# Eight modulation steps move to the first output stage, and two output tiles begin inside the recurrence

## The reference, cut to what matters

```python
mod = silu(cond) @ mod_w[l] + mod_b[l]            # cond: one vector for context, one for latent
sh_a, sc_a, g_a, sh_f, sc_f, g_f = split(mod, 6)
hn = rms_norm(x, norm_mix_g[l]) * (1 + sc_a) + sh_a
out = hybrid_mixer(hn) if l == 0 else rec_mixer(hn)   # l = 1: gated recurrence, 8 heads, two directions
x = x + g_a * out                                 # out ends in a matmul with a 1024 x 1024 matrix
hn = rms_norm(x, norm_ffn_g[l]) * (1 + sc_f) + sh_f
x = x + g_f * expert_choice_ffn(hn)               # each of 16 experts takes its top tokens
```

## Time and profile before

| view | what it gives |
|---|---|
| runs | median 4249.28 us (4249.1 to 4249.85) |
| the profiled execution | own time 4253.98 us, span 4252.2 us |
| PE, matmuls | 3907.3 us busy (92%) |
| DVE | 1762.6 us busy (41%) |
| ACT, POOL | 1120.3 us (26%), 221.8 us (5%) |

### The profile page before, as it was taken

The page is one execution under the profiler, slowest core; times in us unless marked ns, Lnnn a source line. Parts: engine busy times, 40 slices in busy tenths (PEclk is TensorE's granted clock), DMA queues, the critical chain, the costliest instruction groups (busy, mean ns, idle before and its releaser), DMA issues. The chain is left out here.

```text
span 4252.2 us, 56364 instructions
## 1 busy us (share of the span) xinstructions
PE 3907.3 (92%) x24019; PEld 3156.4 (74%) x24019; DVE 1762.6 (41%) x2924; ACT 1120.3 (26%) x2147; POOL 221.8 (5%) x277
## 2 busy tenths in 40 slices
PE   7998989999599999998899999999869599999998
PEld 3443456654499999997788888888744499999997
DVE  3224457755411111111468778888855411111112
ACT  3000024533211111100444555444522211110112
POOL 1120000000000000000000000000000000000000
PEclk9999989999799999999899999999979799999999
DMA  5552110013478888884210000110213578888887
GB/s 187 169 207 90 43 50 1 1 54 116 163 244 255 263 254 263 253 257 147 88 28 28 29 29 23 28 34 19 101 58 112 168 246 257 259 255 264 252 257 241
DMA packets 508361, 615.84 MB, mean 145 GB/s; under 512 B 17994, under 2 KB 468220, under 8 KB 502352
## 3 DMA queue, kind: packets, MB, share of 16 engines
q1 hardware_dynamic: 479808, 500.01, 36.5%
q0 software_dynamic: 25056, 101.61, 8.1%
q10 hardware_dynamic: 3248, 10.62, 0.6%
HBM read 559.02 MB, written 53.17 MB: 144 GB/s over the span
## 5 line engine op out<-in xcount | busy, mean ns | idle before, releaser
L1732 PEld LDWEIGHTS moe_pgu<-step_hnT,expert_w 128*128 128x128 f32 x8192 | 1118.0, 191 | 16.5 <-issue 16.5
L1732 PE MATMUL moe_pgu<-step_hnT,expert_w 128*128 128x160 f32 x8192 | 1125.7, 300 | 3.4 <-ACT step_hnT L1772 3.4
L1835 DVE TENSOR_TENSOR moe_hT<-moe_sg,moe_pgu 128x160 f32<-128x160 f32 x256 | 82.2, 321 | 1004.8 <-PE moe_pgu L1732 995.0
L1744 PE MATMUL moe_pol<-expert_w,moe_hT 128*128 128x256 f32 x2048 | 457.5, 381 | 2.3 <-DVE moe_hT L1835 1.0
L2034 PE MATMUL rec_pz<-step_hnT,rec_w 128*128 128x256 f32 x1920 | 424.5, 380 | 3.5 <-ACT l_zc L2106 1.9
L1744 PEld LDWEIGHTS moe_pol<-expert_w,moe_hT 128*128 128x128 f32 x2048 | 383.2, 190 | 59.0 <-DVE moe_hT L1835 9.9
L1783 ACT ACTIVATE moe_sg<-moe_pgu 128x160 f32<-128x160 f32 x256 | 77.8, 304 | 1301.4 <-PE moe_pgu L1732 1301.4
L2034 PEld LDWEIGHTS rec_pz<-step_hnT,rec_w 128*128 128x128 f32 x1920 | 362.7, 191 | 52.0 <-ACT l_zc L2106 2.3
L2038 PE MATMUL rec_pz<-rec_w,step_hnT 128*128 128x256 f32 x1280 | 288.2, 384 | 15.1 <-ACT rec_zg L2109 15.1
L2038 PEld LDWEIGHTS rec_pz<-rec_w,step_hnT 128*128 128x128 f32 x1280 | 243.9, 193 | 50.6 <-ACT rec_zg L2109 17.9
L2064 PE MATMUL rec_pg<-rec_ring 128*128 128x128 f32 x1600 | 196.9, 282 | 47.6 <-DVE rec_AT L2361 19.9
(11 more groups left out here) (391 smaller groups left out, 4456.0 us busy)
## 6 DMA issues: line engine op xcount, KB each, us to landing
expert_w<-in_moe_w_gu SPq DMA_DIRECT2D x256, 1024.0 KB, 10.5
expert_w<-in_moe_w_down SPq DMA_DIRECT2D x128, 1024.0 KB, 13.7
late_w<-in_mod_w POOLq DMA_DIRECT2D x40, 1024.0 KB, 5.2
rec_w<-in_r_w_in SPq DMA_DIRECT2D x40, 512.0 KB, 4.0
scratch_xm<-op_x ACTq DMA_DIRECT2D x20, 512.0 KB, 2.6
scratch_xn<-op_xn POOLq DMA_DIRECT2D x20, 512.0 KB, 5.3
mod_w<-in_mod_w SPq DMA_DIRECT2D x8, 1024.0 KB, 16.7
hin_w<-in_e_w_in SPq DMA_DIRECT2D x12, 512.0 KB, 9.4
```

The source lines that it names most:

```text
L1732: m = nc.tensor.matmul(pgu[2 * (f % 2) + part][:, :], w[j][:, k, (f % 2) * P:(f % 2 + 1) * P], ring[:, k, e % 8, :], start=(k == 0), stop= ...
L1744: m = nc.tensor.matmul(pol[q // 2][:, (q % 2) * SW:(q % 2 + 1) * SW], hT[:, k, 0:CL], w[8 + q][:, k, :], start=(k == 0), stop=(k == KD - 1))
L1835: nc.vector.tensor_tensor(hT[:, f, :], sg[:, f % 2, :], pgu[2 * (f % 2) + 1][:, :], ALU.mult).then_inc(multiplied, 1)
```

## The change

Six things are changed.

1. `hyena_in`: the group (1, 0), `sh_a` and `sc_a` of layer 1, leaves `LATE`. 32 steps stand behind the first 24 of the 27 calls. DVE's `add_bias` follows tiles 4, 6, 8 and 10, and no longer tile 11.
2. `op0` computes that group behind its last tile: eight weight steps and one for the bias, woven into PE's last transposes, logits and routing; the weights come over SP into a ring of four buffers. ACT copies the rows and the columns, DVE clears a PSUM bank and makes the gains.
3. `gate_add` writes its product to `xn` instead of back into PSUM, and PE waits for the product (`products`) instead of the sum (`gated`). The wait for a free `xn` moves from `scale` to `gate_add`.
4. In the recurrence's order projection steps are set apart: steps 4 and 5 of d = 0, and 15 and 16 of d = 1, have one place each before `prod` L16 and before `prod` L8; step 19 stands before `prod_o` instead of behind it.
5. In the last head 28 half tiles of `op1` (k = 0 to 6 of its first two tiles) are put into PE's order: 20 before `prod` L64 of d = 1, four before `prod` L16, four before `prod_o`. Their PSUM banks stay allocated into `op1`.
6. `op1` is called with `begun=2`: its first two tiles do only k = 7, and the transposes of tile 0 stand in tile 2 at k = 2.

The diff, cut (`ORDER` of tiles is renamed `TILES` throughout):

```diff
-LATE = [(0, 1), (0, 2), (1, 0), (1, 1), (1, 2)]
+LATE = [(0, 1), (0, 2), (1, 1), (1, 2)]
-LATE_CALLS = 27
+LATE_CALLS = 24
@@ hyena_in, PE
-                        for n in range(NLATE * call // LATE_CALLS, NLATE * (call + 1) // LATE_CALLS):
+                        for n in range(NLATE * call // LATE_CALLS, min(NLATE, NLATE * (call + 1) // LATE_CALLS)):
                             modulate(n)
-                        if call % 6 == 2 and call >= 8:
+                        if call in (8, 14, 20):
@@ hyena_in, DVE
-                if tile in (5, 7, 9, 11):
+                if tile in (5, 7, 9):
                     columns((tile - 5) // 2)
-                if tile in (4, 6, 8, 10, 11):
+                if tile in (4, 6, 8, 10):
                     add_bias((tile - 3) // 2)
@@ out_proj_route, SP
+            def load_mod(n):
+                if n >= 4:
+                    sp.wait_ge(mod_used, n - 3)
...
+                sp.dma_start(ring[n % 4][:, :, :].rearrange("p j n -> p (j n)"), src).then_inc(mod_in[n % 4], 16)
+            if shift_of:
+                load_mod(0)
+                load_mod(1)
             sp.wait_ge(mm, NT)
+            if shift_of:
+                for n in range(2, KD + 1):
+                    load_mod(n)
             for j in range(4, 9):
                 load_expert(sp, A, layer, expert_w, expert_w_in, j, 0)
@@ out_proj_route, PE
+            def modulate(n):
+                if n == 0:
+                    pe.wait_ge(sums_zero, 2)
+                pe.wait_ge(mod_in[n % 4], 16 * (n // 4 + 1))
+                for j in range(4):
+                    m = nc.tensor.matmul(sums[32 * j:32 * j + 2, :], S["scond"][:, :, n] if n < KD else pick[:, :], ring[n % 4][:, j, :],
+                                         start=(n == 0), stop=(n == KD), tile_position=(0, 32 * j))
+                m.then_inc(mod_used if n < KD else summed, 1)
-                    pe.wait_ge(gated, n - 1)
-                for k in range(KD):
+                    pe.wait_ge(products, n - 1)
+                for k in range(KD - 1 if n < begun else 0, KD):
+                    if begun and (n, k) == (2, 2):
+                        transposes(0)
...
+            modulate(0)
+            modulate(1)
             transposes(NT - 1)
+            modulate(2)
+            modulate(3)
             logits(2)
+            modulate(4)
             to_tokens(2)
+            modulate(5)
             to_experts(2)
+            for n in range(6, KD + 1):
+                modulate(n)
+            if shift_of:
+                pe.wait_ge(mod_row, 1)
+                for q in range(4):
+                    m = nc.tensor.transpose(columns[:, q * P:(q + 1) * P], row[:, q * P:(q + 1) * P], S["ident"][:, :])
+                m.then_inc(mod_tr, 1)
@@ out_proj_route, DVE
-                nc.vector.tensor_tensor(psm[n % 2][:, :], psm[n % 2][:, :], gate[...], ALU.mult).then_inc(products, 1)
+                if n >= 2:
+                    dve.wait_ge(tr, n - 1)
+                    dve.wait_ge(xn_stored[n % 2], 16 * (n // 2))
+                nc.vector.tensor_tensor(xn[:, n % 2, :], psm[n % 2][:, :], gate[...], ALU.mult).then_inc(products, 1)
-                nc.vector.tensor_tensor(x[:, n % NB, :], psm[n % 2][:, :], x[:, n % NB, :], ALU.add).then_inc(gated, 1)
+                nc.vector.tensor_tensor(x[:, n % NB, :], xn[:, n % 2, :], x[:, n % NB, :], ALU.add).then_inc(gated, 1)
...
             gate_add(9)
+            if shift_of:
+                nc.vector.memset(sums, 0.0).then_inc(sums_zero, 1)
...
+            if shift_of:
+                dve.wait_ge(mod_col, 1)
+                gains_of(nc, S, shift_of, 0)
@@ out_proj_route, ACT, behind exponentials(2)
+            if shift_of:
+                act.wait_ge(summed, 1)
+                nc.scalar.activation(row[:, :], sums, ACT.Copy).then_inc(mod_row, 1)
+                act.wait_ge(mod_tr, 1)
+                for j in range(4):
...
+                r.then_inc(mod_col, 1)
             act.wait_ge(b_ready, 1)
@@ rec_order
+        if last:
+            halves = [(h, ("w", n, c, k)) for n, c in ((0, 0), (0, 1), (1, 0), (1, 1)) for k in range(RH - 1)]
+            for before, part in ((L64, halves[0:20]), (L16, halves[20:24])):
+                x = o.index((h, ("prod", 1, before)))
+                o[x:x] = part
-        o += [(h + 1, ("p", n)) for n in tail[0] if not last] + here(("prod_o",))
+        o += [(h + 1, ("p", n)) for n in tail[0] if not last] + (halves[24:] if last else []) + here(("prod_o",))
-        ps0 = [[0], [1], [2], [3], [4, 5], [], [], [9, 10], [6, 7, 8]]
+        ps0 = [[0], [1], [2], [3], [4], [5], [], [9, 10], [6, 7, 8]]
-... [[11], [12], [13], [14], [15, 16], [], []], [[17, 18], [19, 20, 21], [22, 23, 24]])
+... [[11], [12], [13], [14], [15], [16], []], [[17, 18, 19], [20, 21], [22, 23, 24]])
@@ recurrence, PE
+                elif kind == "w":
+                    n, c, k = tok[1:]
...
+                    pe.wait_ge(op_w_in[k], 16)
+                    pe.wait_ge(yr_in[k], 16)
+                    nc.tensor.matmul(bank[:, :], hnT[:, k, TILES[n] * P:(TILES[n] + 1) * P], op_w(k)[:, c * 512:(c + 1) * 512],
+                                     start=(k == 0), stop=False)
```

More of the change, by code:

```diff
@@ L659, in columns @@
                 columns_of(nc, S, layer, g, late[q % 2]).then_inc(col_out, 1)
-                if (layer, g) != (0, 1) and (layer, g) != (1, 1):
+                if g == 2:
                     dve.wait_ge(col_out, q + 1)
-                    gains_of(nc, S, layer, 0 if g == 0 else 1)
+                    gains_of(nc, S, layer, 1)
             normed(0)
@@ L1248, in load_expert @@
     sp.dma_start(w[j][:, :, :], src.rearrange("(k p) n -> p k n", p=P)).then_inc(w_in[j], 16)
-ORDER = list(range(CT, NT)) + list(range(CT))
+TILES = list(range(CT, NT)) + list(range(CT))
 PHASES = [(0, 4), (4, 4), (8, 2)]
@@ L1257, in out_proj_route @@
 def out_proj_route(nc, A, S, tag, w, w_in, early_gate, lhs, lhs_in, x_in, x_out, layer, hnT, xn_dram, router, idx, idx_four, gates,
-                   expert_w, expert_w_in):
+                   expert_w, expert_w_in, begun=0, begun_psm=None, shift_of=None):
     NB = 3
@@ L1284, in out_proj_route @@
         ssq, rstd = fixed("ssq", [P, NT], ROUTE_AT + 11936), fixed("rstd", [P, NT], ROUTE_AT + 12000)
-        psm = [ps(f"psm{i}", [P, D]) for i in range(2)]
+        psm = begun_psm or [ps(f"psm{i}", [P, D]) for i in range(2)]
         pst = ps("pst", [P, D])
@@ L1298, in out_proj_route @@
         GB = CAP[1] // 8
+        if shift_of:
+            ring = [fixed(f"mod{i}", [P, 4, 512], ROUTE_AT + 12064 + 8192 * i if i < 2 else EARLY["op0_w"] + 8192 * (i - 2)) for i in range(4)]
+            row = fixed("mod_row", [P, 512], EARLY["op0_w"] + 3 * 8192)
+            pick = fixed("mod_pick", [P, 2], EARLY["op0_w"] - 8 * 1024 - 64)
+            sums, columns = psm[0][:, 0:512], psm[1][:, 0:512]
+            mod_in = [sem(f"mod_in{i}") for i in range(4)]
+            sums_zero, mod_used, summed, mod_row, mod_tr, mod_col = (sem(n) for n in "sums_zero mod_used summed mod_row mod_tr mod_col".split())
         def tokens(n):
-            return slice(ORDER[n] * P, (ORDER[n] + 1) * P)
+            return slice(TILES[n] * P, (TILES[n] + 1) * P)
         @block.sync
@@ L1378, in _ @@
                         to_experts(0)
-                    if n and k == (3 if n == 8 else 5):
+                    if begun and (n, k) == (2, 2):
+                        transposes(0)
+                    if n and (n != 1 or not begun) and k == (3 if n == 8 else 5):
                         transposes(n - 1)
@@ L1409, in gate_add @@
                 dve.wait_ge(mm, n + 1)
-                nc.vector.tensor_tensor(psm[n % 2][:, :], psm[n % 2][:, :], gate[:, 0 if ORDER[n] < CT else 1, :], ALU.mult).then_inc(products, 1)
+                if n >= 2:
+                    dve.wait_ge(tr, n - 1)
+                    dve.wait_ge(xn_stored[n % 2], 16 * (n // 2))
+                nc.vector.tensor_tensor(xn[:, n % 2, :], psm[n % 2][:, :], gate[:, 0 if TILES[n] < CT else 1, :], ALU.mult).then_inc(products, 1)
                 dve.wait_ge(products, n + 1)
                 dve.wait_ge(x_ins[n % NB], 16 * (n // NB + 1))
-                nc.vector.tensor_tensor(x[:, n % NB, :], psm[n % 2][:, :], x[:, n % NB, :], ALU.add).then_inc(gated, 1)
+                nc.vector.tensor_tensor(x[:, n % NB, :], xn[:, n % 2, :], x[:, n % NB, :], ALU.add).then_inc(gated, 1)
             def scale(n):
@@ L1536, in to_hnT @@
             def to_hnT(n):
-                c = 0 if ORDER[n] < CT else 1
+                c = 0 if TILES[n] < CT else 1
                 act.wait_ge(tr, n + 1)
@@ L1565, in _ @@
             exponentials(2)
+            if shift_of:
+                act.wait_ge(summed, 1)
+                nc.scalar.activation(row[:, :], sums, ACT.Copy).then_inc(mod_row, 1)
+                act.wait_ge(mod_tr, 1)
+                for j in range(4):
```

(23 more changed lines are left out.)

24 lines of the change are left out of this document (14 added, 10 removed).

## The result

The changed kernel takes 4197.99 us (median of four runs, 4197.36 to 4208.02) against 4249.57 beside it (4249.1 to 4256.5): 51.6 us less, a ratio of 0.988 with a 95% interval of 0.9862 to 0.9898. The forecast was 45.1 less and 4204; the time lies in the range of 4190 to 4228, and the gain is larger than forecast.

What follows compares the result with a forecast made beforehand. PE was taken to bound the kernel, its matmuls filling 92% of the span. The terms -6.3 - 8.2 + 2.0 + 0 - 7.5 - 2.5 - 22.6 gave -45.1 us, from 4249.28 to 4204.2; range 4190 to 4228.

Steps and rivals of the forecast that it cites:

- A, fewer steps: Input projection: six fewer modulation steps on PE before the last call and slightly shorter ring waits, -6.3 us.
- A, the gap: End of the input projection: 9.5 us idle before the convolution shrinks once POOL's last store is earlier, -8.2 us.
- B: End of `op0`: nine modulation steps mostly hidden in PE's idle time, with some delay and DVE work showing, +2.0 us.
- The rival on the ring: End of `op0`: steps 4 and 5 wait for weights and hold the last transposes, +8 us, 4212; chance 0.07.
- C: `gate_add`'s product in `xn`: earlier release gives nothing, as PE never waits for a sum in `op1`, 0 us.
- D: Recurrence: projection steps set apart shorten seven heads' waits (-5) and remove some clock drops (-2.5), -7.5 us.
- The other moves: Recurrence, steps 4 | 5 and 15 | 16: their place only changes which product waits for DVE, 0 us.
- The slower rival (DVE binding): Recurrence: moved steps delay products for which DVE then waits, +57.5 us, 4269; chance 0.04.
- E: Last head: half tiles fit PE's idle time at no cost, and later products run at a higher clock, -2.5 us.
- the rival on the clock: Last head: half tiles run at half clock and overflow the idle time, +20 us and no clock gain, 4227; chance 0.10.
- F: `op1`: 28 halves of 0.85 us leave PE, less a stall in tile 2, -22.6 us.
- The stall of 1.2: `op1`, tile 2: transposes of tiles 0 and 1 share one PSUM buffer that ACT must empty, 1.2 us.

Runs made afterwards that it cites:

- the late store on POOL and on SP: Changed kernel with the input projection's last store of modulation rows waiting for DVE's last columns: 4208.78 us from POOL's queue, 4206.97 from SP's.
- mod_behind: Changed kernel with all nine modulation steps of `op0` moved behind the routing, none before the last transposes and logits: 4208.68 us.
- begun_undone: Changed kernel without half tiles in the last head and without begun tiles in `op1`: 4227.7 us.
- mod_alone: Kernel before with only the moved modulation steps; product, recurrence order, half tiles and begun tiles as before: 4236.41 us.
- room: Changed kernel with eight useless half-tile-sized matmuls added behind the twenty halves before `prod` L64 of the last head: 4199.07 us.
- halves_left_out: Changed kernel with the 28 half tiles left out and nothing in their place, `op1` still called with `begun=2`: 4204.74 us.
- tails_undone: Changed kernel with projection step 19 back behind `prod_o`: 4210.62 us.

## Why the prediction was right, point by point

- **A, fewer steps**: -6.3 forecast, -7.0 measured between the same two events, as the mean of two and twelve profiles.
- **A, the gap**: -8.2 forecast, 9.47 to 0.89, -8.6. The cause was argued from two neighbours in time; the late store on POOL and on SP shows it.
- **B**: +2.0 forecast, +0.2 to +0.4 measured for the whole stage (`op0` 207.27 with the modulation alone, 207.53 here, 207.1 before). Mis-sized: the steps before the logits were counted as a delay only. With them the granted clock is at 1.00 for the logits in place of 0.50, the logits fell from 3.6 to 1.8 us, and that paid for the clearing, the gains and the steps. The prediction had this as a bound (-1), not as the likely case, and expected DVE's wait to stay at 3 to 5 us. From PE's last half tile to its last routing step (L1447, before L1401) it takes 40.4 us here and 41.5 before, so the end of the stage got shorter; in four experiments with the same end it takes 39.7 to 39.8, and their `op0` 205.0 to 205.4. What is longer in the whole stage lies ahead of it: behind a wait of 4.72 for DVE, which was there before, five records of a tile's 32 run at the lower clock here and two in the profile of before (eight records from 1040.91 on in 5.76 us, with 0.50 granted from 1041 to 1044; eight from 1058.25 on in 4.47, with 0.50 granted from 1058.3 to 1059.2). The rival on the ring is real, but only where the order leaves no cover: `mod_behind` pays 10.
- **C**: 0 forecast; 0 in `op0`. In `op1`, with its two short tiles, it saves 0.8 to 0.9.
- **D**: -7.5 forecast, -12.2 measured. The terms were right, their size not: seven waits gave 0.84 each, where 0.7 was taken, and all three clock falls went (5.1), where 2.5 was taken; 1.2 come from the clock in the last head, which the forecast did not have. The other moves gave nothing, as forecast. The slower rival (DVE binding) did not show beyond 0.4 us in a head, DVE's wait for `prod_o`:

```profile
DVE rec_y L2456 <- PE rec_pg L2162: 2.9, 7, 0.4
```

- **E**: -2.5 forecast for a higher clock behind the halves; 3.3 between the profiles, 2.4 and 3.7 in the two kernels without halves. The halves ran at a granted clock of 1.00 (3048.7 to 3065.8 us; the rival on the clock fell); the product waits 1.03 for DVE behind them, near the 0.86 of the sum.
- **F**: -22.6 forecast, -24.9 to the start of the fourth tile, 23.3 in `begun_undone`. The stall of 1.2 was 0.29, and the first matmuls lose less at low clock, 0.50 granted in their first 2 us in the three kernels (eight records in 5.35 in place of twelve in 8.41, or in 6.86 in `begun_undone`).

D and E overlap: undone one at a time they lengthen the recurrence by 12.2 and 3.9 us, undone together (`mod_alone`, 1103.60 against 1089.17) by 14.4, where 10.0 was forecast. So the terms miss by 1.1 in A, 1.6 in B, 4.4 in D with E, and 0.7 to 2.3 in F. All go one way, and their sum of 7.8 to 9.4 lies between the 6.5 us by which the medians' gain exceeds the forecast of 45.1 and the 11.5 by which the profiled executions' does. No term's miss hid another's.

## What to carry to other kernels

A DMA of GpSimd's queue that is awaited right before a barrier is a candidate for moving away from it, or to another queue, even if it is tiny: the four stores of 4 KB here cost 8.6 us, and from such a store's start to the next stage 3.18 us passed with SP's queue against 10.67 with POOL's. Its price is read in the gap between the last busy engine and the next stage. Work put into PE's idle time is to be counted twice, once for the room that it needs and once for the clock of the next products: here 20 records that took 4.61 us at 0.51 granted took 2.40 at 1.00 with eight more matmuls ahead of them (`room`), and the last head took 2.4 us more without the halves (`halves_left_out`). The projection step that waited for a copy was cheaper where the copy had been made: its wait cost 2.16 us in place of 1.37 for another and, in three heads of seven, 1.7 more for the clock behind it.

## What the runs showed beyond that

The falls of the clock behind the wait of 2.16 us repeat: three of seven heads in both profiles of before, in `mod_alone` and in `tails_undone`, always the first and the third and then the sixth or the seventh. One and the same wait so costs 2.16 us in one head and about 3.9 in another. And 6.87 us of useless matmuls in the last head cost only 1.4, the rest coming back as waits and clock.
